# Keys, softmax and one wait moved in the cross-attention of a two-block decoder kernel

## What is computed

```python
mixed = jnp.concatenate([y_ssd, y_mla], axis=-1) @ w_out[l]      # y_mla: 8 heads of 128
x = x + mixed
h = rms_norm(x, xattn_norm_g[l]);  m = rms_norm(mem, mem_norm_g[l])
# memory_cross_attention, X_HEADS = 4, X_HEAD_DIM = 128
q = rms_norm((h @ w_q).reshape(bsz, seq, 4, 128), q_norm_g)
k = rms_norm((m @ w_k).reshape(bsz, mlen, 4, 128), k_norm_g)
v = (m @ w_v).reshape(bsz, mlen, 4, 128)
s = jnp.einsum('bshd,bmhd->bhsm', q, k) * 128 ** -0.5
p = jax.nn.softmax(s, axis=-1)
o = jnp.einsum('bhsm,bmhd->bshd', p, v)
x = x + o.reshape(bsz, seq, 512) @ w_o
```

## Time and profile before

| | before |
|---|---|
| median of 3 runs | 3523.42 us (3523.11 to 3524.86) |
| profiled execution, its own time | 3520.93 us |
| span of its profile | 3519.1 us |
| busy: PE, DVE, ACT | 98%, 60%, 49% |
| mean granted clock of TensorE | 0.998 |

### The profile page before, as it was taken

One profiled execution on the slowest core, in us unless ns is written; L12 is line 12 of the kernel. 1 busy time (PEld: TensorE's weight loads), 2 busy tenths in 40 slices (PEclk: granted clock), 3 DMA queues, 4 the chain that ended last, 5 costly groups with the idle time before them and its releaser, 6 DMA issues.

```text
span 3519.1 us, 43525 instructions
## 1 busy us (share of the span) xinstructions
PE 3456.8 (98%) x18590; PEld 2968.8 (84%) x18590; DVE 2107.8 (60%) x2188; ACT 1717.3 (49%) x2024; POOL 22.7 (1%) x42
## 2 busy tenths in 40 slices
PE   7999999999999999999999999999999999999999
PEld 6888888888888888888888888888898888888887
DVE  6766667554656866655545545577666555555454
ACT  4743464356555465554434434445755644344343
POOL 1000000000000000000000000000000000000000
PEclk9999999999999999999999999999999999999999
DMA  6554554554555444445555555554445455555554
GB/s 236 197 178 142 194 199 163 198 183 168 193 178 183 174 147 153 166 146 180 191 191 191 191 192 190 185 175 171 150 144 180 144 192 189 194 186 188 194 188 167
DMA packets 88578, 630.91 MB, mean 179 GB/s; under 512 B 10064, under 2 KB 10304, under 8 KB 13248
## 3 DMA queue, kind: packets, MB, share of 16 engines
q1 hardware_dynamic: 85104, 611.75, 50.4%
q0 software_dynamic: 3280, 16.36, 1.3%
HBM read 625.98 MB, written 2.10 MB: 178 GB/s over the span
## 4 chain that ended last, share of the span: by engine, by line
PE 81%; DVE 9%; ACT 5%; DMA 3%; issue 1%; DVEq 0%; POOL 0%; ACTq 0%; POOLq 0%
PE G L547 25%; PE G L549 12%; PE G L539 12%; PE G L541 12%; PE G L540 12%; DVE w_lo L459 4%; ACT w_hi L451 3%; DMA w_raw<-in_s_gate 1%; PE G L531 1%; PE G L532 1%; PE G L533 1%; PE M L825 1%; DVE arena L769 1%; PE M L1153 1%; DMA w_raw<-in_s_ssd 1%
## 5 line engine op out<-in xcount | busy, mean ns | idle before, releaser
L459 DVE TENSOR_TENSOR w_lo<-w_raw,w_hi 128x2048 fp32r<-128x2048 f32 (+1 forms) x585 | 1327.7, 2272 | 1220.0 <-ACT w_hi L451 1219.4
L451 ACT ACTIVATE w_hi<-w_raw 128x2048 fp32r<-128x2048 f32 (+1 forms) x585 | 1110.8, 1899 | 1558.1 <-PE G L549 701.4
L547 PE MATMUL G<-x_halves,w_hi 128*128 128x512 f32 x4256 | 1345.2, 397 | 20.1 <-DVE w_lo L459 16.3
L549 PEld LDWEIGHTS G<-x_halves,w_lo 128*128 128x128 f32 x4256 | 801.0, 188 | 186.2
L549 PE MATMUL G<-x_halves,w_lo 128*128 128x256 f32 x4256 | 841.4, 279 | 0.0
L547 PEld LDWEIGHTS G<-x_halves,w_hi 128*128 128x128 f32 x4256 | 650.2, 189 | 24.9 <-issue 14.6
L539 PE MATMUL G<-w_hi,y_halves 128*128 128x512 f32 x1648 | 649.2, 394 | 6.1 <-DVE y_halves L1128 2.6
L541 PE MATMUL G<-w_hi,y_halves 128*128 128x512 f32 x1648 | 642.9, 390 | 0.0
L540 PE MATMUL G<-w_lo,y_halves 128*128 128x512 f32 x1648 | 642.5, 390 | 0.0
L539 PEld LDWEIGHTS G<-w_hi,y_halves 128*128 128x128 f32 x1648 | 309.8, 188 | 70.9 <-DVE y_halves L1128 4.4
L541 PEld LDWEIGHTS G<-w_hi,y_halves 128*128 128x128 f32 x1648 | 309.6, 188 | 64.8
(11 more groups left out here) (445 smaller groups left out, 2686.3 us busy)
## 6 DMA issues: line engine op xcount, KB each, us to landing
w_raw<-in_s_up SPq DMA_DIRECT2D x176, 1024.0 KB, 4.9
w_raw<-in_s_down SPq DMA_DIRECT2D x88, 1024.0 KB, 4.9
w_raw<-in_s_ssd SPq DMA_DIRECT2D x40, 1024.0 KB, 4.9
w_raw<-in_s_hgrn SPq DMA_DIRECT2D x32, 1024.0 KB, 4.9
w_raw<-in_s_gate SPq DMA_DIRECT2D x32, 1024.0 KB, 4.9
w_raw<-in_s_mlstm SPq DMA_DIRECT2D x32, 1024.0 KB, 4.9
w_raw<-in_s_mlstm_gate SPq DMA_DIRECT2D x32, 1024.0 KB, 4.8
w_raw<-in_s_lru SPq DMA_DIRECT2D x16, 1024.0 KB, 5.1
```

The lines of the kernel that those rows point to most:

```text
L451: act.activation(whi[p % SETS][:, 0:n_], raw[p % RAW][:, 0:n_], ACT.Copy).then_inc(S("hi_ready"), 1)
L459: dve.tensor_tensor(wlo[p % SETS][:, 0:n_], raw[p % RAW][:, 0:n_], whi[p % SETS][:, 0:n_].bitcast(F32), ALU.subtract).then_inc(S("lo_ready ...
L547: pe.matmul(o, hi[:, k, f], x2, start=first, stop=False, skip_group_check=True)
L549: mm = pe.matmul(o[:, 0:T], lo[:, k, f], x2[:, 0:T], start=False, stop=last, skip_group_check=True)
```

## The change

Three edits, the same in both layers:

- The first chunk of `out_b` asks for seven heads at k-block 6 and for the eighth at k-block 7. Before, it asked for all eight at k-block 6.
- On ACT, `key_roots` moves from place 4 (behind the high half of piece 7) to 3.25, right behind the keys' eviction. On DVE, `key_scaled` moves from 4 to 3.5, ahead of the low half of piece 7.
- On ACT and DVE, the softmax of head 0 moves from place 7 to the end of place 6, behind `query_roots(0)` and `query_scale(0)`, and so ahead of the halves of piece 10. The softmax of head 2 moves from place 9 to the end of place 8, ahead of the halves of piece 12.

No instruction is added or taken away apart from one wait on `att_out` in each layer.

```diff
-            plans[f"out_b{l}"][0].need = {0: ("att_out", 12 * l + 4), 4: ("att_out", 12 * l + 6), 6: ("att_out", 12 * l + 8)}
+            plans[f"out_b{l}"][0].need = {0: ("att_out", 12 * l + 4), 4: ("att_out", 12 * l + 6), 6: ("att_out", 12 * l + 7),
+                                          7: ("att_out", 12 * l + 8)}
...
-            at(4, key_roots)
-            at(6, lambda: query_roots(0))
-            at(7, lambda: softmax(0))
+            at(3.25, key_roots)
+            at(6, lambda: query_roots(0), lambda: softmax(0))
             at(7.5, lambda: softmax(1))
-            at(8, lambda: query_roots(1), lambda: att_turn_act(act, 0, xa["pt"], False, l))
-            at(9, lambda: att_turn_act(act, 1, xa["pt"], False, l), lambda: softmax(2), lambda: softmax(3))
+            at(8, lambda: query_roots(1), lambda: att_turn_act(act, 0, xa["pt"], False, l), lambda: softmax(2))
+            at(9, lambda: att_turn_act(act, 1, xa["pt"], False, l), lambda: softmax(3))
...
-            at(4, key_scaled)
+            at(3.5, key_scaled)
             at(5, key_out)
-            at(6, lambda: query_scale(0))
-            at(7, lambda: softmax(0))
+            at(6, lambda: query_scale(0), lambda: softmax(0))
             at(7.5, lambda: softmax(1))
-            at(8, lambda: query_scale(1))
-            at(9, lambda: softmax(2), lambda: softmax(3))
+            at(8, lambda: query_scale(1), lambda: softmax(2))
+            at(9, lambda: softmax(3))
```

## The result

| | before | with the change |
|---|---|---|
| median | 3523.27 us (3522.81 to 3525.59, 6 runs) | 3510.23 us (3508.36 to 3512.01, 6 runs) |
| ratio | | 0.9965, 95% interval 0.9955 to 0.9974 |
| profiled execution: time, span | 3520.93, 3519.1 | 3512.01, 3510.2 |
| granted clock, mean | 0.998 | 0.999 |

What follows compares the result with a forecast made beforehand. TensorE, at work for 98% of the span, was taken as the bound, so only its gaps and slow stretches could give. Savings of 4.4 + 5.8 + 2.8 = 13.0 from 3523.42 gave 3510.4 us, range 3507.0 to 3516.0.

Steps and rivals of the forecast that it cites:

- Part 1: First chunk of out_b: asking for the last head one k-block later saves 1.4 us a layer, 2.8 in all.
- Part 2: Before the key turn: a wait of 1.11 us goes, a new one before the column sums leaves 0.29.
- Part 3: Before head 0's turn and the second column sums: earlier softmax 0 removes waits of 1.18 and 1.5 us.
- Part 4: Second column sums to middle of piece 9: clock no longer falls, saving 1.6 us in layer 0, 3.0 in layer 1.
- The first rival: Clock still falls, where it did (3513.0 us) or behind the new wait at the values (3513.6 to 3516.4); chance 0.15.
- Part 5: Earlier softmax 2: the wait at 1545.65 goes, saving 0.83 us; a new wait of 1.0 comes before the values.
- The sum: Whole kernel: 4.4 us from layer 0, 5.8 from layer 1 and 2.8 from out_b make 13.0 saved.
- The two new waits: On TensorE in each layer: about 0.8 us idle before the first column sums, about 1.0 before the first values matmul.

Runs made afterwards that it cites:

- the version with all repairs: Changed kernel plus keys' way back earlier on DVE, values' eviction before head 3's softmax on ACT, heads 0 and 1 output halves before piece 13's: 3503.98 us, ratio 0.995.

## Why the prediction was right, point by point

**Part 1, out_b: right.** Forecast 1.4, measured 1.37 by itself and in the change.

**Part 2, keys: right in the mechanism, too high in size.** The step that a queue behind the high half of piece 8 holds the query squares was right: 0.80 idle, where about 0.8 was foretold. The net was forecast at 0.29 and is about 0.1: the column sums came 18.55 behind piece 4 instead of the assumed 18.45, and the matmuls behind the new wait start slower (3.76 from column sums to scores against 3.68). I had allowed for that slower restart in part 1 and forgot it here. The two timed comparisons agree: with the like falls X is 62.55 and 60.98 with this edit and 62.64 and 61.08 without.

**Part 3, softmax 0: right.** Both waits went, and by the run with this edit alone it carries the whole gain of X. The one term that was off: I gave the scores 0.7 from start to visible; with the change DVE's maximum starts 1.13 behind the scores (1516.88 and 1518.01). That and the later column sums put the high half of piece 10 at 1521.18, which is 1519.46 counted as in the trace before (piece 4 starts 1.72 later here), 0.49 behind the 1518.97 that I had put, and with it the chain down to the values. TensorE waits for that chain, so it decides: the first values matmul comes at 1544.94 on the same count, where 1544.55 was forecast. Those 0.39 are most of what X in layer 0 falls short (3.94 against 4.4); besides, the matmuls behind that wait start 0.10 slower.

**Part 4, clock: right for this change, for a reason stated too firmly.** The sizes fit (1.6 and 3.0; measured 1.61 and 2.97), with 0.11 of each being restart: with both gaps and no fall, in the first run of the keys' edit, the stretch takes 3.87 (1526.97 to 1530.84). In X the fall is worth a little less, 1.33 and 2.90 (60.98 and 62.55 against 59.65 with the same code), since without it TensorE waits 0.84 and not 0.67 before the turn of head 2. "The pair has one in both layers" rested on two cases of one execution; the runs show a fall in some nine executions of ten. The gain of the medians contains it nearly in full, since the median execution has the fall. The rule of the Trainium skill (TensorE: Matmul & The Clock Gate, "Why this matters for your kernels") is to leave no idle gaps between bursts of matmuls, or the half rate comes back; but it means gaps longer than either of these. By that rule 1.03 and 1.28 would bring no fall; in four of the five profiles that have this pair close together the trace shows one, so the measurement goes further than the page. The first rival, that the new wait of 1.07 at the values would do the same, has nothing for it: the clock was at 1.00 behind it in all the profiles, and behind one of 1.60 too.

**Part 5, softmax 2: right, and not drawn to its end.** Forecast: 0.83 won, 1.0 lost. The chain from high half 10 to the values' eviction was foretold at 24.7 (1518.97 to 1543.70) and took 24.6 (1521.18 to 1545.79). Those two terms say that the edit loses 0.2; the run without it says 0.48, because the new wait costs more than the 1.0 that I had put. I reported both terms and summed them without saying that the change would be better without this part. The table load took its 1.28 with the ACTIVATE 0.02 behind it:

```profile
1534.94 1.28 ACT L1070 ACT_TABLE_LOAD   x1
1536.24 0.56 ACT L1070 ACTIVATE arena<-M,small 128x256 f32<-128x256 f32 x1
```

So the switch of 2.66 us that the Trainium skill states (ScalarE: Activation LUTs, "What ACT_TABLE_LOAD costs") did not show on the chain: here the trace differs from the page, since only 0.02 lies between the two rows.

**The sum.** By the stretches 13.0 was forecast and 11.96 came, so the terms were 1.0 too high; the medians say 13.04. The hit to 0.2 us is luck in that size, since the start of the kernel varies by more. The two new waits are what was put too small. By starts I had 0.82 and 0.97 for them. The first is 0.96 (the column sums 18.55 behind piece 4, and 17.59 without the wait), the second 1.23 (4.53 from the turn of head 2 to the values, and 3.30 in the version with all repairs), and behind them the matmuls start 0.08 and 0.10 slower. These four make 2.37, which is what that version gains in X (2.38).

## What to carry to other kernels

In an engine that runs its queue in order, ask of each wait which item in front of the awaited one could stand behind it, and then follow the other engine to its next wait: of the 1.1 won at the key turn 0.1 was left, and a softmax moved ahead turned a wait of 0.67 into one of 1.07. Fix the next wait in the same edit, as the version with all repairs does, and count a new wait as dear as an old one: by starts, with the slower matmuls behind it. Sum up each part of a change by itself, since a part that loses hides well beside one that wins ten times as much. And time a stretch between two fixed matmuls, where tenths of a microsecond can be read from one execution while the totals scatter by 4 and more (3508.34 to 3512.66 for the changed kernel).

## What was not expected of the hardware

Two idle gaps of about 1.2 and 1.5 us (1.03 and 1.28 as idle time in the profile) with a few small transposes between them bring TensorE's clock from 2.4 to 1.2 GHz in most executions, at a cost of about 4.2 us in X for the two layers together, and in a few executions not at all. With a whole piece of matmuls between gaps of about the same size the clock stayed up in the one execution seen. In all four profiles with the fall it came in both layers, and from the column sums to the scores of head 2 one of them took some 1.6 and the other 3.0 to 3.1 more than the changed kernel; which one changed between executions of the same kernel.
